# Second experts of a two-block transformer: residual and scaled shared rows as starting accumulators, six down buffers, another order of steps, one program block to the end

## The reference

```python
h = rms_norm(x, g_ffn_norm[l]) * (1.0 + scale_f) + shift_f
x = x + gate_f * moe_ffn(h, w_router[l], ...)
return rms_norm(x, g_final)

# moe_ffn: top 6 of 64 experts (in 4 of 8 groups) for each token, width 256
hb = jax.nn.silu(xb @ w_exp_gate[e]) * (xb @ w_exp_up[e])
yb = (hb @ w_exp_down[e]) * g[:, None]      # for blocks of rows of one expert
routed = segment_sum(yb, row_tok)
shared = (jax.nn.silu(xf @ w_sh_gate) * (xf @ w_sh_up)) @ w_sh_down
return shared + routed
```

## Time and profile before

| | |
|---|---|
| median of 3 runs | 1918.8 us (1913.86 to 1923.05) |
| the profiled execution's own time | 1919.48 us |
| its span, first to last instruction | 1917.4 us |
| mean granted TensorE clock over the span | 0.922 |
| TensorE / VectorE / ScalarE / GpSimd busy | 86% / 33% / 24% / 25% |
| share of the 16 DMA engines taken by the SP queue | 55.0% |
| expert stage, first row gather to last down product | 1249 to 1866 us |
| from the last down product to the end of the span | 52 us |

### The profile page before, as it was taken

The page is one execution under the profiler, slowest core; times in us unless marked ns, Lnnn a source line. Parts: engine busy times, 40 slices in busy tenths (PEclk is TensorE's granted clock), DMA queues, the critical chain, the costliest instruction groups (busy, mean ns, idle before and its releaser), DMA issues. The chain is left out here.

```text
span 1917.4 us, 22063 instructions
## 1 busy us (share of the span) xinstructions
PE 1645.2 (86%) x8000; PEld 905.6 (47%) x8000; DVE 630.7 (33%) x1602; ACT 458.2 (24%) x984; POOL 478.3 (25%) x385
## 2 busy tenths in 40 slices
PE   6989999899999968999999969979877887877880
PEld 3434446773333326678778756444333333323330
DVE  1775516441111106651644234512111111111115
ACT  2412216321111105652642122111111110101111
POOL 4997907001111106740200000012111111111100
PEclk9799999989999988999999979989898998889895
DMA  5353410548999954412212265458999999999954
GB/s 197 132 186 110 157 63 5 220 169 340 405 406 404 402 151 144 173 64 88 94 45 88 92 238 197 174 178 311 397 384 377 379 376 353 368 368 399 355 180 139
DMA packets 112343, 446.23 MB, mean 233 GB/s; under 512 B 20356, under 2 KB 26900, under 8 KB 74856
## 3 DMA queue, kind: packets, MB, share of 16 engines
q1 hardware_dynamic: 96360, 411.13, 55.0%
q0 software_dynamic: 15840, 33.60, 7.0%
q10 hardware_dynamic: 32, 0.04, 0.0%
HBM read 427.33 MB, written 44.10 MB: 246 GB/s over the span
## 5 line engine op out<-in xcount | busy, mean ns | idle before, releaser
L1993 PE MATMUL bank<-big,heads 128*32 128x512 f32 (+2 forms) x944 | 259.4, 659 | 47.5 <-DMA big<-in_w_exp_up_dram 41.6
L1993 PEld LDWEIGHTS bank<-big,heads 128*32 128x32 f32 (+2 forms) x944 | 81.8, 140 | 147.6 <-issue 147.1
L2044 DVE SCALAR_TENSOR_TENSOR heads<-heads,small,bank 128x256 f32<-128x256 f32 x39 | 18.7, 480 | 391.2 <-ACT heads L2096 391.2
L2283 POOL DMA_INDIRECT acc_scratch<-heads,small x55 | 87.2, 1586 | 231.4 <-DVE heads L2076 131.6
L460 PE MATMUL bank<-big,h_cols 128*128 128x512 f32 x320 | 143.3, 602 | 0.3 <-ACT heads L610 0.3
L2124 POOL DMA_INDIRECT heads<-h_scratch,small x39 | 40.4, 1035 | 379.6 <-DVE small L2061 341.6
L1993 PE MATMUL bank<-h_cols,heads 128*32 128x512 f32 (+1 forms) x256 | 80.5, 687 | 34.1 <-DMA big<-in_w_exp_up_dram 34.1
L1175 PE MATMUL bank<-causal,ident 128*128 128x512 f32 x178 | 92.9, 671 | 15.6 <-PEq L178 15.6
L2029 PE MATMUL bank<-h_rows,heads 128*32 128x512 f32 (+2 forms) x336 | 103.4, 613 | 0.6 <-ACT heads L2090 0.6
L2096 ACT ACTIVATE heads<-bank 128x256 f32<-128x256 f32 x39 | 15.0, 384 | 370.8 <-PE bank L1993 370.8
L818 POOL TENSOR_SCALAR junk_and_spare<-junk_and_spare,cond 128x512 f32<-128x512 f32 x56 | 97.4, 1740 | 5.5
(11 more groups left out here) (476 smaller groups left out, 3199.3 us busy)
## 6 DMA issues: line engine op xcount, KB each, us to landing
big<-in_w_exp_gate_dram SPq DMA_DIRECT2D x65, 1024.0 KB, 16.3
big<-in_w_exp_up_dram SPq DMA_DIRECT2D x65, 1024.0 KB, 26.8
h_rows<-in_w_exp_down_dram SPq DMA_DIRECT2D x40, 1024.0 KB, 25.1
big<-in_w_in_dram SPq DMA_DIRECT2D x13, 2048.0 KB, 8.7
junk_and_spare<-in_w_mod_dram SPq DMA_DIRECT2D x24, 1024.0 KB, 5.4
big<-in_w_exp_down_dram SPq DMA_DIRECT2D x24, 1024.0 KB, 20.8
junk_and_spare<-in_w_exp_gate_dram SPq DMA_DIRECT2D x16, 1024.0 KB, 19.0
junk_and_spare<-in_w_exp_up_dram SPq DMA_DIRECT2D x16, 1024.0 KB, 30.5
```

Source lines behind the costliest of these rows:

```text
L1993: mm = pe.matmul(b_au[b][tile, :], xt[:, b, P * c + tile.start:P * c + tile.stop], gu[places[n][0]][:, :, c, :], start=c == 0, stop=c == K ...
L2283: return pool.indirect_dma_start(out=acc, out_offset=bass.IndirectOffsetOnAxis(at, 0), in_=rows, in_offset=None, bounds_check=acc.shape[0] ...
```

## The change

1. `keep_rows=K.acc2_dram`: the residual rows are stored as the start of the upper accumulator, before each store of normed rows. The shared expert's rows start the lower one, whose zero stores are gone. GpSimd multiplies the shared expert's down weights by `K.gain` beforehand (`scale_down`), and TensorE waits for that.
2. VectorE copies both halves of every step's rows out of PSUM and multiplies them by `K.gain` on the way; ScalarE no longer takes part.
3. Six down buffers: the memory of `K.x` holds two of them. They are loaded before the shared expert's gate and up are done (`into_residual`).
4. SP issues loads step by step: after gate and up of step i, the gate-up loads of the buffers it freed; after down of step i-1, its down loads.
5. A group of seven steps is now b a b b a b b. The last two steps are shared ones.
6. GpSimd waits for the accumulators' start only ahead of its first row addition, no longer ahead of the gathers. `keep_clock` runs 3 matmuls for 5.
7. One block holds expert steps, overflow and end. SP reads both accumulators at the end, VectorE adds them. The multiplications at the end are gone.

```diff
@@ output_and_ranks, sync
-                if keep_rows:
-                    sp.wait_ge(added, T + t + 1)
-                    sp.dma_start(K.acc_dram[P * t:P * t + P, :], K.x[:, t, :]).then_inc(K.acc_set, 16)
+                sp.wait_ge(added, T + t + 1)
+                sp.dma_start(keep_rows[P * t:P * t + P, :], K.x[:, t, :]).then_inc(K.acc_set, 16)
...
             if shared:
+                sp.wait_ge(K.acc_set, 16 * T)
+                preload.into_residual(sp)
                 shared.gate_up_done(sp)
@@ expert_steps
-        steps += [b[0], b[1], a[0], b[2], b[3], b[4], a[1]]
+        steps += [b[0], a[0], b[1], b[2], a[1], b[3], b[4]]
@@ SortedWeights
-    GATE_UP, DOWN = 6, 4
+    GATE_UP, DOWN = 6, 6
@@ shared_expert
     def down(pe, between):
         w = w_down
-        pe.wait_ge(down_in, 16)
+        pe.wait_ge(scaled, 1)
...
+    def scale_down(pool):
+        pool.wait_ge(down_in, 16)
+        pool.wait_ge(K.final_in, 32)
+        pool.tensor_tensor(w_down, w_down, K.gain[:, :].unsqueeze(1).broadcast_to([P, FH, D]), ALU.mult).then_inc(scaled, 1)
@@ sorted_experts_stage, vector
-                    dve.tensor_copy(ys[:, b, 0:512], b_y[0][:, :]).then_inc(y_dve, 1)
-            dve.wait_ge(K.acc2_lower, 32 * T)
-            for t in range(T):
-                step(dve.tensor_tensor(lower[:, t, :], lower[:, t, :], K.gain[:, :], ALU.mult))
-                step(dve.tensor_tensor(K.x[:, t, :], K.x[:, t, :], lower[:, t, :], ALU.add))
+                    for half in range(2):
+                        cols = slice(512 * half, 512 * half + 512)
+                        dve.tensor_tensor(ys[:, b, cols], b_y[half][:, :], K.gain[:, cols], ALU.mult).then_inc(y_taken, 1)
+            overflow.vector(dve, overflow.register(dve))
+            final.vector(dve)
@@ gpsimd
-            pool.wait_ge(K.acc_stored, 16 * T)
-            pool.wait_ge(K.acc2_lower, 16 * T)
...
+                    if i == 1:
+                        pool.wait_ge(K.acc_set, 16 * T)
+                        pool.wait_ge(K.acc_stored, 16 * T)
@@ sync
+            weights.down(sp, 4)
+            weights.down(sp, 5)
+            for i in range(N):
+                if gate_up_freed(i):
+                    sp.wait_ge(au_mm, i + 1)
+                for n in gate_up_freed(i):
+                    weights.gate_up(sp, n)
+                if i >= 1 and down_freed(i - 1):
+                    sp.wait_ge(y_mm, i)
+                    for n in down_freed(i - 1):
+                        weights.down(sp, n)
+            overflow.sync(sp, overflow.register(sp), (y_mm, N))
+            sp.wait_ge(scattered, 16 * N)
+            final.sync(sp)
@@ final
+            dve.wait_ge(rows_in[t], 32)
+            dve.tensor_tensor(K.hr[:, t, :], K.hr[:, t, :], lower[:, t, :], ALU.add).then_inc(added, 1)
...
+            for place, first in ((K.hr, 0), (lower, S)):
+                sp.dma_start(place[:, t, :], K.acc2_dram[first + P * t:first + P * t + P, :]).then_inc(rows_in[t], 16)
```

More of the change, by code:

```diff
@@ L1290, in _ @@
                 shared.scalar(act)
+        @block.gpsimd
+        def _(pool):
+            if shared:
+                shared.scale_down(pool)
         @block.vector
@@ new lines, in scalar, with body @@
+    def scalar(act, most):
+        def body(e, b, n):
+            for half in range(2):
+                act.wait_ge(xt_mm, 2 * n + 1 + half)
+                act.activation(xt[:, 512 * half:512 * half + 512], K.bank[1 + half][:, :], ACT.Copy)\
+                   .then_inc(xt_copied, 1)
+            act.wait_ge(au_mm, n + 1)
+            act.activation(silu, K.bank[3][:, 0:FE], ACT.Silu).then_inc(silu_ready, 1)
+            act.wait_ge(ht_mm, n + 1)
+            act.activation(hidt, K.bank[5][:, 0:FE], ACT.Copy).then_inc(ht_copied, 1)
+            if row is None:
@@ new lines, in gpsimd, with body @@
+    def gpsimd(pool, most, done=None):
+        def body(e, b, n):
+            pool.wait_ge(idx_ready, 2 * n + 2)
+            pool.sem_inc(row_dmas, 1)
+            pool.indirect_dma_start(out=xg, out_offset=None, in_=K.h_dram,
+                                    in_offset=bass.IndirectOffsetOnAxis(idx, 0), bounds_check=S - 1,
+                                    oob_is_err=False).then_inc(gathered, 16)
+            pool.wait_ge(y_taken, 2 * n + 2)
+            pool.sem_inc(row_dmas, 1)
+            scatter_add(pool, acc, ys, idx).then_inc(scattered, 16)
+            pool.wait_ge(scattered, 16 * n + 16)
+        each(pool, most, body, done)
@@ new lines, in sync @@
+    def sync(sp, most, done=None):
+        with sp.If(most > first):
+            if done:
+                sp.wait_ge(*done)
+            with sp.Fori(0, E, 1) as e:
+                for g, w in enumerate((w_gate, w_up)):
+                    sp.dma_start(gu[:, g, :, :], w[one(e)].rearrange("e (p c) f -> (e p) c f", p=P)).then_inc(gu_in, 16)
+                sp.dma_start(dn, w_down[one(e)].rearrange("e (p j) d -> (e p) j d", p=P)).then_inc(d_in, 16)
+                sp.wait_ge(y_mm, NL * e + NL)
+                sp.sem_inc(experts_done, 1)
+            sp.wait_ge(scattered, 16 * E * NL)
@@ new lines, in final, with scalar, vector @@
+    lower = K.big[:, 8192:12288].rearrange("p (t d) -> p t d", t=T)
+    def scalar(act):
+        step = K.act.on(act)
+        for t in range(T):
+            act.wait_ge(added, t + 1)
+            step(act.activation(K.big[:, 1024 * t:1024 * t + 1024], K.hr[:, t, :], ACT.Square, accum_out=ss[:, t:t + 1]))
+            act.activation(sd[:, t:t + 1], ss[:, t:t + 1], ACT.Sqrt, scale=1.0 / D, bias=K.eps[:, 0:1]).then_inc(std, 1)
+    def vector(dve):
+        step = K.dve.on(dve)
+        for t in range(T):
+            dve.wait_ge(rows_in[t], 32)
+            dve.tensor_tensor(K.hr[:, t, :], K.hr[:, t, :], lower[:, t, :], ALU.add).then_inc(added, 1)
+        for t in range(T):
+            dve.wait_ge(std, t + 1)
+            step(dve.reciprocal(rs[:, t:t + 1], sd[:, t:t + 1]))
+            dve.scalar_tensor_tensor(out=K.hr[:, t, :], in0=K.hr[:, t, :], scalar=rs[:, t:t + 1], in1=K.shift[:, :],
+                                     op0=ALU.mult, op1=ALU.mult).then_inc(ready, 1)
@@ new lines, in sync @@
+    def sync(sp):
+        for t in range(T):
+            for place, first in ((K.hr, 0), (lower, S)):
+                sp.dma_start(place[:, t, :], K.acc2_dram[first + P * t:first + P * t + P, :]).then_inc(rows_in[t], 16)
+        for t in range(T):
+            sp.wait_ge(ready, t + 1)
+            sp.dma_start(K.out[0, P * t:P * t + P, :], K.hr[:, t, :]).then_inc(stored, 16)
+        sp.wait_ge(stored, 16 * T)
+    parts = State()
+    parts.scalar, parts.vector, parts.sync = scalar, vector, sync
@@ L3192 @@
+    return parts
 FIRST_BLOCK = [("setup", setup), ("norm1", first_norm), ("mix", mixers),
```

260 lines of the change are left out of this document (103 added, 157 removed).

## The result

| | before | after |
|---|---|---|
| median (4 runs each) | 1918.2 us (1913.9 to 1923.1) | 1888.5 us (1888.0 to 1890.8) |
| ratio to before | 1 | 0.984, 95% interval 0.982 to 0.986 |
| span of the profiled execution | 1917.4 us | 1889.1 us |
| first row turn to last down product | 1257.3 to 1865.5: 608.2 us | 1259.4 to 1854.9: 595.5 us |
| from there to the end of the span | 51.9 us | 34.2 us |

The gain is 30 us where 57 were forecast; the time lies just outside the range. By the profiles, 28.3 us: +2.1 at the start, -12.7 in the stage of the experts, -17.7 behind it. The forecast had -3.3, -36.6 (its terms 2, 3 and 4) and -17.5. The stage begins at another time in every profile: at 1254.1 to 1257.3 us in the three profiled kernels that start like the one before, at 1254.6 to 1259.4 in the nine that start like the changed one, so the +2.1 of this pair is known to a few us only.

The account below looks back on a forecast made before the run. The prediction took DMA transfers, not quite full because SP's queue blocks, to set the pace from 1340 to 1840 us; -3.3 - 5.1 - 22 - 9.5 - 17.5 = -57.4 from 1919.5 gave 1862 us, range 1845 to 1887.

Parts of the forecast that it names:

- terms 2, 3 and 4: Expert stage: two down blocks loaded before the steps (-5.1 us), gaps closed (-22), shorter end of the steps (-9.5).
- 1. The start: Start of the expert stage: earlier gathers against a delay of VectorE's router by GpSimd's multiplication, net -3.3 us.
- The gathers' 8.3 us: At the start: gathers no longer wait for the shared rows' stores, so TensorE begins 8.3 us earlier.
- the collision: At the start: GpSimd's multiplication of the shared weights holds VectorE's router, charged 5.0 us of delay.
- term 3: Steady stretch from 1340 to 1840 us: six down buffers and new queue order close the DMA gaps, -22 us.
- The deeper buffers were used: Denies a rival (6%): SP stays blocked in issuing, so new loads come no sooner; 1889 us.
- term 4: End of the steps: the last down product comes 9.4 us behind the last transfer, not 18.9; -9.5 us.
- The first rival: Steady stretch: the transfers' mean rate is the limit, so filling gaps slows other stretches; 1884 us, chance 14%.
- a falling rate in full stretches: Steady stretch: a sign that the prediction is wrong, if the transfer rate in full stretches falls.
- 5. The end: From the last down product to the end: 34.4 us where it was 51.9, -17.5 us.
- 6. The rest: Later row additions, 39 fewer ScalarE copies and two fewer `keep_clock` matmuls: claimed off the path, no time counted.
- Row additions did not become the chain: Denies a rival (3%): row additions, each waiting for the one before, set the steps' pace; 1949 us.

Follow-up runs that it names:

- placed_halves: The changed kernel with GpSimd's multiplication of the shared down weights cut in two halves, each released at a MAX8 and MATCH_REPLACE8 row of VectorE's router; 1879.0 us.
- before_downward: The kernel before, with every second part of a step filled with its expert's rows from the last row down, nothing else changed; 1894.3 us.
- rows_downward: The changed kernel with every second part of a step filled with its expert's rows from the last row down; 1863.0 us.
- no_additions: The changed kernel without its 39 row additions, GpSimd only counting the semaphore, so the output lacks the routed experts; 1800.0 us.

## Why the forecast was wrong

- **1. The start (-3.3; +2.1).** The gathers' 8.3 us were right, as `placed_halves` shows, and so was the collision in kind (3.7 us of the 5.0 charged). Missing was what a late VectorE does to TensorE: "TensorE needs it at 1220, so that wait is free" looked at the weights alone, while the hidden rows come from the delayed VectorE. TensorE stood idle for 4.94 us and then ran at half speed, which cost the gathers 5 to 6 us more. So 8.3 us were gained and 9.6 lost; the rest of the +2.1 is that the router itself began 0.9 us later in this profile (1202.91 for 1202.04).
- **2 to 4. The stage (-36.6; -12.7).** This is the step that failed, term 3 above all (-22). "Free transfer time in it is 24.5 us" took the mean over 16 engines for the state of each, and the dips to 0.69 were put down to SP's blocked queue alone. The fullest engine had by the sum 448.6 + 304 x 0.493 = 598 us of work in a stage of 608: some 10 us of slack, not 36, whatever the queue does; 12.7 were won. `before_downward` shows the same from the other side: with the queue still blocked for 283.7 us, evener rows alone bring the share to 1.01. The deeper buffers were used, the queue did run with few waits, but the rate stayed at 375 GB/s. The reading that fits is that the engines with fewer rows only ran ahead of the fullest and then waited for it; no view of the profile names the engine of a transfer. The plateau at 0.3 stands where term 4 expected TensorE's last wait to be short. The first rival ("the mean rate is the limit", 1884 us) came within 5 us of the time by a wrong mechanism: the same kernel moves 394 GB/s with its rows filled from both ends. That it came close is luck. Even engines would not have saved the forecast either: there the stage falls by 16.9 us (584.7 to 567.8), not by 36.6. One of the forecast's own signs did tell: it named a falling rate in full stretches, and 398 GB/s at a share of 1.02 became 375 at 1.00.
- **5. The end (-17.5; -17.7).** Right in size, and in its steps within 1 us: the last row addition had landed 10.7 us behind the last down product (10.9 forecast), and the whole took 34.2 (34.4).
- **6. The rest.** No run took these parts back alone. Row additions did not become the chain: from 1340 to 1800 us GpSimd stood before 28 of 29 of them for VectorE's rows (98.1 us in all), not for the landing of the one before.

That the fullest engine is a floor is shown by fillings that change nothing but which place a row has; which engine serves which place is inferred from them, and fits. Why the weights' reads among uneven engines take longer on record in the changed kernel (400 MB per ms, for 416 in `rows_downward`: 160.0 MB in 83.7% of 460 us; 542 reads of over 400 ns for 118) is not shown.

## What to carry to other kernels

A share over 16 DMA engines is a mean: where indexed transfers skip places, count what each engine gets, since the fullest one can set the pace, and closing gaps for the others then wins little (12.7 us here of 36.6 forecast). Look at how a burst of loads ends: a plateau at a fraction of the engines is a hint, though no proof, since `rows_downward` ends with shares of 0.4 to 0.5 too. The proof is to move the rows to other places and see whether the time follows. And when one engine is delayed, ask whether TensorE runs idle behind it; that idle time and the clock that falls after it can cost more than the delay (5 to 6 us for 3.7 here).

## What was not expected of the hardware

- Filling the places of indexed transfers from both ends was worth 25 us of 1888, without a byte less.
- One added row costs an engine 0.33 us (0.493 less 0.164), twice a gathered one. Both are means of the transfers' own times, from `no_additions` and the changed kernel.
- Gaps in the mean share of the DMA engines went by evener rows alone, with the issuing queue blocked as long as ever (`before_downward`: a share of 1.01 for 0.97, 283.7 us of waits for 281.8).
- GpSimd's multiplication also held VectorE operations with one input tile (a TENSOR_SCALAR of 128x32, 2.46 us for 0.18), but not a TENSOR_REDUCE that ran beside it for 0.42 us as ever, nor the MAX8 and MATCH_REPLACE8 under `placed_halves`. The Trainium skill (SBUF — State Buffer, SBUF: two separate sides) names two-input operations and those in a two-port mode as the ones that are held; the runs agree, if TENSOR_SCALAR counts among the latter.
- 394 GB/s in `rows_downward` and 417 from 1340 to 1700 us in `no_additions`, on one core; the Trainium skill (DMA: Bandwidth & Descriptors, Bandwidth) has some 358 for each of two cores that read at once and more for one alone. These runs agree with the second part; none shows the first. The prediction cited the 358 for one core and, with 373 GB/s in its own trace, rightly gave that rule no weight.
